# Hybrid decoder layer: blocks of two heads taken tile by tile, their mixing matmuls issued alternately

## The reference

```python
# MoBA, per head: softmax over causal blocks with a T5 bias
p = jax.nn.softmax(logits, axis=-1).astype(v.dtype)
return (jnp.einsum('bhqnk,bhqnkd->bhqd', p_sel, v_sel)
        + jnp.einsum('bhqk,bhkd->bhqd', p_own, v_own))
...
# retention, per head
scores = jnp.einsum('bhcnd,bhcmd->bhcnm', qc, kc) * decay_mask[None, :, None]
y_inner = jnp.einsum('bhcnm,bhcme->bhcne', scores, vc)
```

## Time and profile before

| | us |
|---|---|
| median of 2 runs | 705.71 (705.66 to 705.76) |
| span of the profiled execution | 703.6 |
| one loop turn of the mixer | 67.3 |
| PE busy | 691.9 |
| DVE busy | 363.3 |
| ACT busy | 299.8 |
| POOL busy | 130.8 |

### The profile page before, as it was taken

The page is one execution under the profiler, slowest core; times in us unless marked ns, Lnnn a source line. Parts: engine busy times, 40 slices in busy tenths (PEclk is TensorE's granted clock), DMA queues, the critical chain, the costliest instruction groups (busy, mean ns, idle before and its releaser), DMA issues.

```text
span 703.6 us, 9375 instructions
## 1 busy us (share of the span) xinstructions
PE 691.9 (98%) x3210; PEld 536.2 (76%) x3210; DVE 363.3 (52%) x538; ACT 299.8 (43%) x485; POOL 130.8 (19%) x113
## 2 busy tenths in 40 slices
PE   7999999999999999999999999999999999999996
PEld 7877667766775666578998888888888888887885
DVE  3334325722672267478675455555555564472445
ACT  5456316622662265165453343334333443363341
POOL 4534514431543243032200000000000000000002
PEclk9999999999999999999999999999999999999999
DMA  9523211321132122256333333334333222341223
GB/s 283 176 91 91 90 61 31 90 89 60 39 92 78 60 89 87 93 188 196 97 89 90 107 91 99 89 90 119 90 89 92 88 60 63 106 145 46 89 89 119
DMA packets 87110, 69.15 MB, mean 98 GB/s; under 512 B 2265, under 2 KB 76169, under 8 KB 87090
## 3 DMA queue, kind: packets, MB, share of 16 engines
q1 hardware_dynamic: 85618, 63.62, 30.0%
q0 software_dynamic: 1472, 5.26, 2.0%
HBM read 66.76 MB, written 2.12 MB: 98 GB/s over the span
## 4 chain that ended last, share of the span: by engine, by line
PE 95%; ACT 1%; DMA 1%; POOL 1%; DVE 0%; issue 0%; SPq 0%; DVEq 0%; POOLq 0%; ACTq 0%
PE bank L432 80%; PE bank L576 3%; PE bank L513 3%; PE bank L566 2%; PE bank L504 2%; PE bank L556 2%; PE bank L503 1%; PE bank L555 1%; DMA raw<-in_w_in_dram 1%; PE bank L443 1%; POOL ws L350 0%; ACT ws L768 0%; ACT hT L775 0%; PE bank L541 0%; PE bank L530 0%; PE bank L523 0%
## 5 line engine op out<-in xcount | busy, mean ns | idle before, releaser
L432 PE MATMUL bank<-hT,ws 128*128 128x512 f32 (+1 forms) x1872 | 416.1, 378 | 1.1 <-DVE hT L1064 0.6
L432 PEld LDWEIGHTS bank<-hT,ws 128*128 128x128 f32 x1872 | 327.2, 189 | 66.7 <-issue 4.6
L432 PE MATMUL bank<-ws,yT 128*128 128x512 f32 x720 | 167.8, 392 | 0.3 <-PE bank L432 0.3
L432 PEld LDWEIGHTS bank<-ws,yT 128*128 128x128 f32 x720 | 133.9, 188 | 29.9 <-issue 2.1
L768 ACT ACTIVATE ws<-raw 128x1024 fp32r<-128x1024 f32 x88 | 92.6, 1053 | 20.6 <-PE bank L432 17.5
L350 POOL TENSOR_TENSOR ws<-raw,ws 128x1024 fp32r<-128x1024 f32 x30 | 75.3, 2510 | 93.4 <-ACT ws L768 93.2
L1048 DVE TENSOR_TENSOR ws<-raw,ws 128x1024 fp32r<-128x1024 f32 x58 | 70.6, 1219 | 6.3 <-ACT ws L768 6.0
L340 POOL TENSOR_SCALAR meansq<-osum 128x1 f32<-128x1 f32 x8 | 3.8, 469 | 371.4 <-ACT work L1001 351.5
L1322 DVE TENSOR_TENSOR ws<-raw,ws 128x1024 fp32r<-128x1024 f32 x22 | 26.9, 1224 | 51.2 <-ACT ws L1008 51.2
L985 ACT ACTIVATE gains<-bank,conv 128x512 f32<-128x512 f32 x22 | 17.2, 781 | 75.0 <-PE bank L432 75.0
L1112 DVE TENSOR_TENSOR work<-bank,work 128x512 f32<-128x512 f32 (+3 forms) x32 | 15.7, 491 | 61.1 <-PE bank L504 61.1
(11 more groups left out here) (110 smaller groups left out, 534.6 us busy)
## 6 DMA issues: line engine op xcount, KB each, us to landing
raw<-in_w_up_dram SPq DMA_DIRECT2D x44, 512.0 KB, 3.8
raw<-in_w_in_dram SPq DMA_DIRECT2D x28, 512.0 KB, 3.9
raw<-in_w_down_dram SPq DMA_DIRECT2D x22, 512.0 KB, 3.8
raw<-in_w_out_dram SPq DMA_DIRECT2D x16, 512.0 KB, 3.3
xs<-in_x_dram SPq DMA_DIRECT2D x4, 512.0 KB, 6.5
work<-bias_vectors POOLq DMA_DIRECT2D x4, 512.0 KB, 5.6
work<-in_decay_dram POOLq DMA_DIRECT2D x4, 512.0 KB, 4.0
out_dram<-work SPq DMA_DIRECT2D x4, 256.0 KB, 2.1
```

Of the source, the lines that this page charges most:

```text
L432: return nc.tensor.matmul(dst, st, mv, start=start, stop=stop)
```

## The change

Blocks are numbered tile by tile instead of head by head. Before, block u was head u // 4, tile u % 4 (retention: 3 - u % 4). Now it is head u % 2, tile u // 2 (retention: 3 - u // 2). Scores, bias, exponential, normalisation, transposes and copies stay one block to a slot, in the new order. The mixing matmuls are issued for a pair of blocks, both heads of one tile. In MoBA they stand in slots u = 4, 6, 8, 10, and for each of the qt + 1 tiles head 0's matmul is followed by head 1's. In retention they stand in r = 3, 5, 7 and u = 0 (tail: 3, 5, 7, 9), head 0's then head 1's. `a_pv` counts pairs. No arithmetic is added or taken away.

```diff
+        def moba_block(u):
+            return u % 2, u // 2
+        def ret_block(u):
+            return u % 2, 3 - u // 2
...
-            def ret_mix(k, u):
-                h, mt = u // 4, 3 - u % 4
...
+            def ret_mix(k, pair):
+                mt = ret_block(2 * pair)[1]
...
-                pe.wait_ge(r_decayed, 8 * k + u + 1)
-                ins = nc.tensor.matmul(bank[YR_BANK][HD * h:HD * h + HD, SEQ - width(mt):SEQ],
-                                       vRrow[:, mt, HD * h:HD * h + HD], retp[:, h, packed(mt):packed(mt) + width(mt)],
-                                       start=mt == 3, stop=mt == 0)
+                pe.wait_ge(r_decayed, 8 * k + 2 * pair + 2)
+                for h in range(2):
+                    ins = nc.tensor.matmul(bank[YR_BANK][HD * h:HD * h + HD, SEQ - width(mt):SEQ],
+                                           vRrow[:, mt, HD * h:HD * h + HD], retp[:, h, packed(mt):packed(mt) + width(mt)],
+                                           start=mt == 3, stop=mt == 0)
...
-                pe.wait_ge(a_probsT, 8 * i + u + 1)
+                pe.wait_ge(a_probsT, 8 * i + 2 * pair + 2)
                 for t in range(qt + 1):
-                    ins = nc.tensor.matmul(bank[YA_BANK][HD * h:HD * h + HD, qt * P:(qt + 1) * P],
-                                           vArow[:, 3 - qt + t, HD * h:HD * h + HD],
-                                           probsT[:, u % 2, t * P:(t + 1) * P], start=t == 0, stop=t == qt)
+                    for h in range(2):
+                        ins = nc.tensor.matmul(bank[YA_BANK][HD * h:HD * h + HD, qt * P:(qt + 1) * P],
+                                               vArow[:, 3 - qt + t, HD * h:HD * h + HD],
+                                               probsT[:, h, t * P:(t + 1) * P], start=t == 0, stop=t == qt)
                 ins.then_inc(a_pv, 1)
...
-                        if r >= 2:
-                            ret_mix(i - 1, r - 2)
+                        if r >= 3 and r % 2:
+                            ret_mix(i - 1, r // 2 - 1)
...
-                    if 3 <= u < 11:
-                        moba_mix(i, u - 3, first)
+                    if 4 <= u < 11 and u % 2 == 0:
+                        moba_mix(i, u // 2 - 2, first)
...
                         if v >= 2:
-                            act.wait_ge(a_pv, 8 * i + v - 1)
+                            act.wait_ge(a_pv, 4 * i + v // 2)
```

More of the change, by code:

```diff
@@ L492, in ret_scores @@
             def ret_scores(k, u):
-                h, mt = u // 4, 3 - u % 4
+                h, mt = ret_block(u)
                 if u == 0:
@@ L504, in ret_scores @@
                 nc.tensor.matmul(dst, klR[rows, tile], qsR[rows, h, wide], start=False, stop=True).then_inc(r_scores, 1)
-            def ret_mix(k, u):
-                h, mt = u // 4, 3 - u % 4
-                if u == 0:
+            def ret_mix(k, pair):
+                mt = ret_block(2 * pair)[1]
+                if pair == 0:
                     pe.wait_ge(vR_ready, k + 1)
                     pe.wait_ge(gate_ready, k + 1)
-                pe.wait_ge(r_decayed, 8 * k + u + 1)
-                ins = nc.tensor.matmul(bank[YR_BANK][HD * h:HD * h + HD, SEQ - width(mt):SEQ],
-                                       vRrow[:, mt, HD * h:HD * h + HD], retp[:, h, packed(mt):packed(mt) + width(mt)],
-                                       start=mt == 3, stop=mt == 0)
-                if u == 7:
+                pe.wait_ge(r_decayed, 8 * k + 2 * pair + 2)
[3 more added lines that the diff above has]
+                                           start=mt == 3, stop=mt == 0)
+                if pair == 3:
                     ins.then_inc(r_pv, 1)
@@ L544, in moba_scores @@
             def moba_scores(i, u, first):
-                h, qt = u // 4, u % 4
+                h, qt = moba_block(u)
                 if u == 0:
@@ L558, in moba_turn @@
             def moba_turn(i, u):
-                qt = u % 4
+                qt = moba_block(u)[1]
                 pe.wait_ge(a_probs, 8 * i + u + 1)
@@ L568, in moba_turn, with moba_mix @@
                 ins.then_inc(a_turned, 1)
-            def moba_mix(i, u, first):
-                h, qt = u // 4, u % 4
-                if u == 0 and not first:
+            def moba_mix(i, pair, first):
+                qt = moba_block(2 * pair)[1]
+                if pair == 0 and not first:
                     pe.wait_ge(a_ylo, i)
-                pe.wait_ge(a_probsT, 8 * i + u + 1)
+                pe.wait_ge(a_probsT, 8 * i + 2 * pair + 2)
                 for t in range(qt + 1):
-                    ins = nc.tensor.matmul(bank[YA_BANK][HD * h:HD * h + HD, qt * P:(qt + 1) * P],
-                                           vArow[:, 3 - qt + t, HD * h:HD * h + HD],
-                                           probsT[:, u % 2, t * P:(t + 1) * P], start=t == 0, stop=t == qt)
+                    for h in range(2):
+                        ins = nc.tensor.matmul(bank[YA_BANK][HD * h:HD * h + HD, qt * P:(qt + 1) * P],
+                                               vArow[:, 3 - qt + t, HD * h:HD * h + HD],
+                                               probsT[:, h, t * P:(t + 1) * P], start=t == 0, stop=t == qt)
                 ins.then_inc(a_pv, 1)
@@ L594, in mixer_turn @@
                         if not first:
-                            ret_mix(i - 1, 7)
+                            ret_mix(i - 1, 3)
                         moba_values(i, first)
@@ L670, in _ @@
                     ret_values(k)
-                if r >= 2:
-                    ret_mix(k, r - 2)
+                if r >= 3 and r % 2:
+                    ret_mix(k, r // 2 - 1)
                 if r < 8:
@@ L871, in mixer_turn @@
                         if not first:
-                            act.wait_ge(a_pv, 8 * i)
+                            act.wait_ge(a_pv, 4 * i)
                         act.wait_ge(vA_turned, i + 1)
@@ L877, in mixer_turn @@
                         v = u - 2
-                        w = width(v % 4)
+                        w = width(moba_block(v)[1])
                         act.wait_ge(a_turned, 8 * i + v + 1)
                         if v >= 2:
-                            act.wait_ge(a_pv, 8 * i + v - 1)
+                            act.wait_ge(a_pv, 4 * i + v // 2)
                         nc.scalar.activation(probsT[:, v % 2, 0:w], bank[T_BANK[v % 2]][:, 0:w],
@@ L884, in mixer_turn @@
                     if u < 8:
-                        w = width(u % 4)
+                        w = width(moba_block(u)[1])
                         act.wait_ge(a_biased, 8 * i + u + 1)
@@ L910, in mixer_turn @@
                         split_hi(u // 3 + 5, i, NU)
-                act.wait_ge(a_pv, 8 * i + 8)
+                act.wait_ge(a_pv, 4 * i + 4)
                 nc.scalar.activation(yT[:, 0, i, :] if isinstance(i, int)
@@ L1154, in bias_and_max @@
             def bias_and_max(i, u, first):
-                h, w = u // 4, width(u % 4)
+                h, w = u % 2, width(moba_block(u)[1])
                 if u == 0:
```

## The result

The changed kernel takes 681.12 us (680.94 to 681.29, 2 runs) against 705.71: a ratio of 0.9652, 95% interval 0.9633 to 0.967. Timed again beside the experiments it took 679.97 us, ratio 0.963 (0.9609 to 0.9652).

What follows compares the result with a forecast made beforehand. TensorE's instruction stream was taken to bound the kernel (PE busy 98%): 705.7 - 10.6 (fewer excursions) - 11.3 (alternating halves) + 0.7 (waits) = 684.5 us, with an 8-in-10 range of 681.5 to 697.0 us.

Steps and rivals of the forecast that it cites:

- Pass cost and number: MoBA and retention mixing matmuls: about 0.11 us per 128-column pass, 34.5 us of stream in all, every pass kept.
- Part 1: Mixing groups of MoBA and retention: 32 fewer excursions into the 64-column shape at 0.33 us each, 10.6 us saved.
- Part 2: Mixing passes alternating between array halves: staggered overlap, 2n + 1 pass times for 4n passes, 11.3 us saved.
- a1 and b0: Mix passes ordered a0 a1, b0 b1: a in the lower 64 array columns, b in the upper; neighbours in different halves overlap.
- bound from above: Mixing passes: perfect overlap of everything halves the 34.5 us, saving 17.2 us; better than staggered had chance 0.04.
- Part 3: Possible new waits: L530 in slot 6 waits for ret_norm, 0.23 us in each of three loop turns, 0.7 us.
- Slots 8 and 9: Mix waiting for block 5's copy, turn for block 7's normalise: slack about 0.5 and 1 us, nothing to pay.
- The range: Whole kernel: 681.5 to 697.0 us, meant to hold 8 in 10; the forecast's own range was 681.5 to 688.
- serial: Rival for the mixing passes: halves don't overlap, changing them is free, only Part 1 remains; 695.1 us, chance 0.27.
- drain per half: Rival for the mixing passes: each change of half costs like a change of shape; 706.3 to 721.5 us, chance 0.09.
- late chain: Rival: slot 6's wait is 1.1 us three times and slot 8's joins, adding 3 us; chance within the forecast's 0.44.
- loads in line: Rival: halves' matmuls overlap, but the other half's weights load only after the pass ahead starts; 688.2 us, chance 0.16.

Runs made afterwards that it cites:

- one-half version: The changed kernel with both heads' mixing matmuls writing the lower partition half, using the same 64 array columns: 697.52 us, a loop turn of 65.16 us.
- norm-first version: The changed kernel with POOL waiting for the group norm's last multiplication (ret_norm, on DVE) before its rotary sum, in the three loop turns: 677.83 us.

## Why the prediction was right, and where it was wrong

- **What bounds it**: right. TensorE stays at 98%, and every microsecond gained is stream.
- **Pass cost and number**: right, 0.11 us per 128 columns, 34.5 us in all; the one-half version gives half of it to 0.01 us a turn.
- **Part 1, 10.6 us**: right. Fewer retention groups gave 0.33 us each, and the one-half version's 2.13 us a turn is 8 x 0.33 - 0.51.
- **Part 2, the step that failed**: "a1 and b0 overlap, and b1 and the next a0; a0 and a1 can't". It took TensorE to start passes strictly in program order, so that b0 had to wait until a1 had started, and sized the overlap at 11.3 us. In fact b0 starts 0.007 us after a0, and b's passes run ahead of up to four of a's; a group of 4n passes takes 2n pass times and not 2n + 1. The term is 17.2 us, which the prediction had as the bound from above and gave a chance of 0.04. The mechanism was right (halves overlap, the change between them is free), its size was too small by 5.9 us. That the time came so near the range is luck: the late start hid 1.8 us of this.
- **Part 3, 0.7 us**: the place was right, L530's chain in slot 6, and the size was 1.5 us, 0.51 us three times (60.87 against the norm-first version's 60.36). The arithmetic gave the chain 0.1 us of slack and named what could break it, a DVE instruction slowed by POOL; it was ret_norm itself that was caught. Reckoned as there, from the start of slot 4 at 107.27 us, L1148 would have ended at 7.5 us had it taken 0.69, and not at 8.1, and TensorE came at 8.0: the slack was 0.5 us, and the 0.96 us that POOL cost made the wait. Slots 8 and 9 cost nothing, as said.
- **What nobody had in the sum**: 1.8 us of late start, seen in the trace of one of the two runs that made the median; the other's mean clock was as low.
- The sum by what was measured: 705.7 - 10.6 - 17.2 + 1.5 + 1.8 = 681.2, against 681.12. A loop turn checks it without the start: 67.29 - 2.64 - 4.31 + 0.51 = 60.85, against 60.86 to 60.91.
- **The range**: its lower end, 681.5, doesn't follow from the terms named beside it, 684.5 - 0.7 - 0.6 = 683.2, and full overlap, 677.9 us without waits, was left outside though no row spoke against it.
- **Rivals**: serial is what the one-half kernel is, at 697.5 (695.1 plus 1.5 of waits, and the late start in some of its runs); there was no drain per half; the late chain came to half of its 1.1 us a turn, without slot 8's; loads in line falls, since the loads of both halves overlap as well. The Trainium skill ("TensorE: Matmul & The Clock Gate", Part 3) lets a weight load overlap matmuls in flight only where the row group differs; here both halves use all 128 rows and eight loads of L587 take 0.42 us, one pair every 0.11 us. The measurement decides against the rule for column halves. The Trainium skill's sentence in "TensorEngine Tiling (Array Packing)", Key Properties, that a change of mode drains and a change of tile doesn't, fits the measurements in both parts: 0.33 us and nothing.

Those loads, from the changed kernel's timeline of weight loads:

```profile
116.37 0.42 PEld L587 LDWEIGHTS bank<-work 128*64 128x64 f32 x8 [0.17 <-issue]
```

## What to carry to other kernels

When a kernel bound by TensorE has matmuls that fill half of the array's columns or rows, put the two halves' work into one group: half of their stream goes, and each group of column halves that disappears between full-width matmuls saves another 0.33 us. Fine alternation isn't needed, but no more than four passes of one half should stand together. When slots get shorter, list every wait that had under about 1 us of slack, and take a DVE instruction that may meet POOL at its slow duration (here 1.65 us for 0.69), not at its usual one. Look at the clock behind a long wait as well: behind the tail's 3.6 us it cost 2.5 us more.

## What the runs showed of the hardware that was not expected

- A pass in the free half of the array starts ahead of up to four passes that stand before it in the program, and two fp32 calls, one for each half, run as if issued together (0.007 us apart).
- Weight loads of the two halves overlap too: eight of 0.136 us in 0.42 us.
- Row halves (64 x 128) overlap as column halves do, starts 0.004 us apart, writing different banks.
- A DVE multiplication of 128 x 512 in SBUF takes 0.69 us alone and 1.65 us when it begins 0.19 us after a POOL operation of 1.28 us: it ends 0.56 us after POOL's. A normalisation of 128 x 512 that began 0.04 us ahead of such an operation took 1.61 us and not 0.49.
- After 2.3 us of idling the granted clock fell to 0.50 for some 3 us in one execution, which cost 1.1 us, and stayed at 1.00 after 2.9 us of idling in another of the same kernel; behind an idle stretch of 3.6 us it was 0.50 for 6 us, which cost 2.5 us.
